# Final norm during the last expert, its own rows normed apart and written over, and one search for both token groups

## What is computed

```
def _expert_choice_ffn(h, w_router, w_gate, w_up, w_down):   # once for each token group
    cap = CAP_FACTOR * N // N_EXPERTS                        # 128 of 1024, 64 of 512; 16 experts
    aff = softmax(h @ w_router)
    gate, idx = lax.top_k(aff.T, cap)                        # each expert picks its tokens
    xe = h[idx]
    hid = silu(xe @ w_gate) * (xe @ w_up)                    # 1024 -> 2048
    ye = (hid @ w_down) * gate                               # 2048 -> 1024
    return zeros.at[idx].add(ye)

x = x + _expert_choice_ffn(rmsnorm(x, g_ffn), ...)
y = x * rsqrt(mean(x * x) + 1e-6) * g_final                  # final norm, every token
```

## Time and profile before

| what | value |
|---|---|
| time before, median of 3 runs | 2661.93 us (2661.03 to 2663.06) |
| profiled execution | 2664.18 us, span 2662.4 us |
| TensorE busy | 2515.5 us, 94% of the span |
| VectorE busy | 1731.1 us, 65% |
| ScalarE busy | 1486.1 us, 56% |
| GpSimd busy | 187.2 us, 7% |
| mean granted TensorE clock | 0.974 |
| moved by DMA | 536.65 MB, mean 202 GB/s |

### The profile page before, as it was taken

How to read it: one execution, slowest core, us unless ns; L and a number is a source line. 1 busy time by engine, 2 the same in 40 slices (tenths; PEclk the granted TensorE clock), 3 DMA queues, 4 the chain that set the end, 5 groups by cost and what they waited for, 6 DMA issues and landing times. The chain is left out here.

```text
span 2662.4 us, 42232 instructions
## 1 busy us (share of the span) xinstructions
PE 2515.5 (94%) x15538; PEld 2229.5 (84%) x15538; DVE 1731.1 (65%) x2743; ACT 1486.1 (56%) x2124; POOL 187.2 (7%) x268
## 2 busy tenths in 40 slices
PE   7999999979965999999999999999999999999992
PEld 5888866657755998999989999899998999989991
DVE  6354277765577766767667676676766767667675
ACT  4333277765543565655656556565565655656553
POOL 0000011000001010110101101011010110101100
PEclk9999999989987999999999999999999999999996
DMA  4332132235435676776767767677676776767765
GB/s 151 127 127 90 62 108 92 89 117 184 144 121 184 234 246 227 253 248 232 246 227 253 248 232 246 227 253 248 231 246 227 252 248 231 246 227 253 249 230 209
DMA packets 95484, 536.65 MB, mean 202 GB/s; under 512 B 10608, under 2 KB 15472, under 8 KB 44848
## 3 DMA queue, kind: packets, MB, share of 16 engines
q1 hardware_dynamic: 88016, 509.72, 54.2%
q0 software_dynamic: 7392, 25.96, 4.5%
HBM read 497.89 MB, written 37.75 MB: 201 GB/s over the span
## 5 line engine op out<-in xcount | busy, mean ns | idle before, releaser
L1413 DVE TENSOR_TENSOR ex_w_lo<-ex_w,ex_w_hi 128x2048 fp32r<-128x2048 f32 x387 | 887.0, 2292 | 471.1 <-ACT ex_w_hi L1366 471.1
L1366 ACT ACTIVATE ex_w_hi<-ex_w 128x2048 fp32r<-128x2048 f32 x387 | 739.2, 1910 | 232.2 <-PE ex_down_ps L1517 114.1
L1499 PE MATMUL ex_gate_ps<-ex_xt,ex_w_hi 128*128 128x384 f32 x2048 | 594.3, 360 | 1.5 <-DVE ex_xt L1419 1.5
L1499 PE MATMUL ex_up_ps<-ex_xt,ex_w_hi 128*128 128x384 f32 x2048 | 592.1, 359 | 0.0
L1501 PE MATMUL ex_gate_ps<-ex_xt,ex_w_lo 128*128 128x192 f32 x2048 | 513.8, 251 | 0.0
L1501 PE MATMUL ex_up_ps<-ex_xt,ex_w_lo 128*128 128x192 f32 x2048 | 512.7, 250 | 0.0
L1501 PEld LDWEIGHTS ex_gate_ps<-ex_xt,ex_w_lo 128*128 128x128 f32 x2048 | 392.5, 192 | 0.6
L1501 PEld LDWEIGHTS ex_up_ps<-ex_xt,ex_w_lo 128*128 128x128 f32 x2048 | 391.2, 191 | 0.0
L1499 PEld LDWEIGHTS ex_gate_ps<-ex_xt,ex_w_hi 128*128 128x128 f32 x2048 | 386.0, 188 | 2.3 <-issue 1.7
L1499 PEld LDWEIGHTS ex_up_ps<-ex_xt,ex_w_hi 128*128 128x128 f32 x2048 | 384.6, 188 | 0.0
L1386 ACT ACTIVATE ex_up_low<-ex_up_ps 128x384 f32<-128x384 f32 x128 | 63.0, 492 | 213.6 <-PE ex_up_ps L1501 213.6
(11 more groups left out here) (215 smaller groups left out, 4142.1 us busy)
## 6 DMA issues: line engine op xcount, KB each, us to landing
ex_w<-in_w_experts SPq DMA_DIRECT2D x387, 1024.0 KB, 4.8
pj_w<-in_w_in SPq DMA_DIRECT2D x54, 512.0 KB, 3.4
at_bias<-in_near_bias SPq DMA_DIRECT2D x8, 1536.0 KB, 8.1
pj_x<-in_x SPq DMA_DIRECT2D x12, 512.0 KB, 4.4
o_scratch<-at_o SPq DMA_DIRECT2D x24, 256.0 KB
mx_o<-o_scratch SPq DMA_DIRECT2D x12, 512.0 KB, 4.1
mx_x<-in_x SPq DMA_DIRECT2D x12, 512.0 KB, 4.6
acc_scratch<-mx_x SPq DMA_DIRECT2D x12, 512.0 KB, 5.4
```

Of the source, the lines that this page charges most:

```text
L1366: act.activation(w_hi[:, c % SLOTS, :], w[:, c % SLOTS, :], ACT.Copy).then_inc(hi_w, 1)
L1413: dve.tensor_tensor(w_lo[:, c % SLOTS, :], w[:, c % SLOTS, :], w_hi[:, c % SLOTS, :].bitcast(F32), ALU.subtract).then_inc(lo_w, 1)
L1499: nc.tensor.matmul(out[:, b, 0:2 * CAP], w_hi[:, slot, f], xt[:, k, :, :].rearrange("p h c -> p (h c)"), start=k == 0, stop=False)
```

## The change

It has four parts.

1. **Search.** The 6 sample rounds in `choose` take partitions 0 to 111, so the prompt's rows too, over 512 columns; the columns that the prompt lacks hold -2. Two rounds over the prompt's rows alone follow. `best` and `at` get 144 columns, the prompt's lists lie from column 80 on. The merge works on both groups in one instruction.
2. **First expert.** GpSimd starts its gathers after the first index operation; VectorE waits until both are issued (`ch.gathering`), splits chunk 0, makes the low halves of the gathered rows and only then splits chunks 1 and 2. `gathered` becomes `gathered_s` and `gathered_p`, and TensorE turns the sample rows when they alone are there.
3. **Last expert.** The loops run over 15 experts and the last one is written out. It turns and gathers no next rows. In it SP loads all 12 tiles of `acc` as they are without the last expert (from chunk 9, after the scatters of the expert before), in 8 slots, ScalarE squares them, VectorE norms them, SP stores them: a schedule by chunk (`FIN_...`).
4. **The last expert's own rows.** GpSimd gathers their `acc` rows into `x_s` and `x_p`. The two output halves are added to them rather than scattered, multiplied by the gain, squared by halves, scaled by their root, and scattered to `out` over what the tiles' stores wrote, after all stores have landed. The finish block is gone.

```diff
+LISTED = 8 * (EARLY + P_ROUNDS)
+SAMPLE_ROWS, ALL_ROWS, PROMPT_ROWS = (
+    (slice(0, SEG_AT + EXPERTS), S_SEG), (slice(0, SEG_ROWS), S_SEG), (slice(PROMPT_AT, SEG_ROWS), P_SEG))
...
-            pool.memset(route.rows[:, 0, :], 0.0).then_inc(ready, 1)
+            pool.memset(route.rows[:, 0, :], -2.0).then_inc(ready, 1)
...
-    for r in range(early, S_ROUNDS):
-        take_best(dve, route, ch.steps, r - early, False, r)
-    for r in range(P_ROUNDS):
-        take_best(dve, route, ch.steps, late + r, True, r)
+    for r in range(EARLY, rounds):
+        take_best(dve, route, ch.steps, r - EARLY, ALL_ROWS if r < S_ROUNDS else PROMPT_ROWS, r)
...
+    dve.tensor_tensor(route.gates[:], half(0, 0), half(0, 1), ALU.max).then_inc(ch.done, 1)
+    dve.tensor_tensor(ch.mine[:], half(0, 0), half(0, 1), ALU.is_ge).then_inc(ch.compared, 1)
+    dve.tensor_tensor(ch.span[:], half(1, 0), half(1, 1), ALU.subtract).then_inc(ch.compared, 1)
...
+    dve.tensor_tensor(route.index[:, :, 0:EXPERTS], ch.span[:], half(1, 1), ALU.add).then_inc(ch.done, 1)
+    dve.tensor_tensor(route.index[:, :, EXPERTS:], ch.span[:, :, 0:1], half(1, 1)[:, :, 0:1],
+                      ALU.add).then_inc(ch.last_index, 1)
...
+FIN_SLOTS, FIN_BATCH = 8, 6
+FIN_LOAD, FIN_STORE = 9, 19
+FIN_SQUARES = [5, 6, 7, 8, 9, 10, 13, 14, 16, 17, 18, 19]
+FIN_ROOTS = [11, 20]
+FIN_NORMS = [12, 13, 14, 15, 16, 17, 20, 21, 21, 22, 22, 23]
+FIN_LAST = [4, 5]
...
+            for c in range(W_CHUNKS):
+                load_w(LAST, c)
+                if c == FIN_LOAD:
+                    sp.wait_ge(y_free, LAST + START)
+                if 0 <= c - FIN_LOAD < FIN_SLOTS // 2:
+                    load_fin(2 * (c - FIN_LOAD))
+                    load_fin(2 * (c - FIN_LOAD) + 1)
+                if c >= FIN_STORE:
+                    store_fin(c - FIN_STORE)
+                    if c - FIN_STORE >= 2:
+                        load_fin(c - FIN_STORE - 2 + FIN_SLOTS)
+            for t in range(W_CHUNKS - FIN_STORE, TILES):
+                store_fin(t)
+                if t - 2 + FIN_SLOTS < TILES:
+                    load_fin(t - 2 + FIN_SLOTS)
...
+            for i in range(FIN_SLOTS):
+                pool.wait_ge(fin_moved[i], stored_at(TILES - 1 - (TILES - 1 - i) % FIN_SLOTS))
+            pool.wait_ge(rooted, 1)
+            pool.indirect_dma_start(d["out"], bass.IndirectOffsetOnAxis(last_row_s, 0),
+                                    fin[:, FIN_LAST[0], :], None).then_inc(last_out, 16)
+            pool.wait_ge(rooted, 2)
+            pool.indirect_dma_start(d["out"], bass.IndirectOffsetOnAxis(last_row_p, 0),
+                                    fin[0:P_CAP, FIN_LAST[1], :], None).then_inc(last_out, 16)
+            pool.wait_ge(last_out, 32)
...
             choose(dve, route, ch)
-
-            for c in range(AHEAD):
-                split(0, c)
+            dve.wait_ge(ch.gathering, 1)
+            split(0, 0)
             for i in range(FILLS):
                 low_x(0, i)
+            for c in range(1, AHEAD):
+                split(0, c)
...
+            def add_last(k):
...
+                dve.scalar_tensor_tensor(out=y_s[:, c], in0=y_ps[k][0], scalar=last_gate_s, in1=x_s[:, c],
+                                         op0=ALU.mult, op1=ALU.add).then_inc(added_s, 1)
+                dve.wait_ge(y_lowered, n)
+                dve.tensor_tensor(y_p_sum[:], y_ps[k][1][0:P_CAP, :], y_low[:], ALU.add).then_inc(y_summed, 1)
+                dve.wait_ge(y_summed, n + START)
+                dve.scalar_tensor_tensor(out=y_p[:, c], in0=y_p_sum[:], scalar=last_gate_p, in1=x_p[:, c],
+                                         op0=ALU.mult, op1=ALU.add).then_inc(added_p, 1)
...
+                dve.tensor_tensor(fin[:, FIN_LAST[0], c], y_s[:, c], gain[:, c], ALU.mult).then_inc(gained, 1)
...
+                inverse_root(dve, refined, len(FIN_ROOTS) * REFINE, last_ss[:], last_rt[:],
+                             [tmp[:, i, 0:2] for i in range(3)], last_rs[:], 1.0 / D)
+                dve.wait_ge(gained, 2 * HALVES)
+                last = [fin[:, FIN_LAST[0], :], fin[0:P_CAP, FIN_LAST[1], :]]
+                dve.tensor_scalar(last[0], last[0], last_rs[:, 0:1], None, ALU.mult).then_inc(rooted, 1)
+                dve.tensor_scalar(last[1], last[1], last_rs[0:P_CAP, 1:2], None, ALU.mult).then_inc(rooted, 1)
...
-            pe.wait_ge(gathered, 32)
+            pe.wait_ge(gathered_s, 16)
             turn_x(0)
             turn_x(1)
+            pe.wait_ge(gathered_p, 16)
             pe.wait_ge(lo_x, 1)
             turn_x(2)
```

More of the change, by code:

```diff
@@ L1376, in _, with expert @@
                 high_x(0, i)
-            with act.Fori(0, EXPERTS) as e:
+            def expert(e, last=False):
                 spans, halves = e * SPANS, e * HALVES
@@ new lines, in finish_norms @@
+            def finish_norms(c):
+                if c in FIN_ROOTS:
+                    b = FIN_ROOTS.index(c)
+                    tiles = slice(b * FIN_BATCH, (b + 1) * FIN_BATCH)
+                    dve.wait_ge(root, b + 1)
+                    inverse_root(dve, refined, b * REFINE, ss[:, tiles], rt[:, tiles],
+                                 [tmp[:, i, :] for i in range(3)], rs[:, tiles], 1.0 / D)
+                    if b == 0:
+                        dve.wait_ge(const_in, 32)
+                for t in range(TILES):
+                    if FIN_NORMS[t] == c:
+                        x = fin[:, t % FIN_SLOTS, :]
+                        dve.scalar_tensor_tensor(out=x, in0=x, scalar=rs[:, t:t + 1], in1=gain[:], op0=ALU.mult,
+                                                 op1=ALU.mult).then_inc(normed, 1)
@@ L1467, in _ @@
+            with dve.Fori(0, LAST) as e:
+                expert(e)
+            expert(LAST, True)
         @block.tensor
@@ L1607, in program @@
+            with pe.Fori(0, LAST) as e:
+                expert(e)
+            expert(LAST, True)
 def program(nc, d):
```

263 lines of the change are left out of this document (156 added, 107 removed).

## The result

The changed kernel takes **2616.27 us** (median of 4 runs, 2614.47 to 2617.07), the kernel before on the same chip 2662.49 us (2661.03 to 2663.29, 4 runs): a ratio of **0.9824, 95% interval 0.9811 to 0.9836**. The forecast was 2615.4 with a range of 2610 to 2623.

The account below looks back on a forecast made before the run. TensorE bounds the expert loop, so only the two ends can gain: 8.3 + 0.45 + 3.2 + 1.7 + 32.9 = 46.5 us off the profiled 2664.2 gives 2617.7, less 2.3 to the median, 2615.4; range 2610 to 2623.

Parts of the forecast that it names:

- Search, 8.3: Behind the last router tile: six prompt rounds of 1.38 us go, more partitions cost nothing; 8.3 us saved.
- Index arithmetic, 0.45: Before the first gather: six fewer comparisons and index operations of 0.08 us ahead of GpSimd's release; 0.45 us saved.
- First gathers, 3.2: Before the first expert: shorter gather issue beside idle VectorE, sample rows turned without awaiting prompt rows; 3.2 us saved.
- Rival (b): First gather's issue is long by itself, not from splits; only 1.9 us gained there, total 2618; chance 0.07.
- Turns, 1.7: Last expert: TensorE no longer turns rows for an expert that doesn't exist; 1.7 us saved.
- the last expert's extra work at 0: Last expert: added norms, squares and table loads fit the idle time of VectorE and ScalarE; no stall, bound 2 us.
- rival (a): Last expert: mixed reads and writes don't reach 360 GB/s, so DMA is late; total 2622 us; chance 0.11.
- DMA lateness, 0.3: Last expert: late transfers delay the last tile's square and the six norms behind the second root; 0.3 us, bounds 0 and 5.
- the second burst: Chunks 19 to 23 of the last expert: 9.4 MB in 22.7 us; 0.8 us late at 400 GB/s, 3.4 at 360.
- (d): Rival: stores beside weight loads cut the queue to 192 GB/s in the last expert; slower, 2676 us; chance 0.03.
- The tail, 19.0: From ScalarE's last output copy to the end: 19.0 us instead of 52.2, the drain last; 33.2 saved.
- Rival (c): At the end: GpSimd's drain isn't needed or is short; 5.3 us less, total 2610; chance 0.06.

Follow-up runs that it names:

- the control: The changed kernel itself, unedited, run again in the same rounds as the variant with both gains of the end; 2614.93 us, ratio 0.9821.
- SP's wait: Changed kernel with the wait for the last two scatters moved from GpSimd to SP; 2614.5 us, ratio 0.9817.
- doubled stores: Changed kernel with each of the twelve tile stores done a second time, to a scratch of its own; 2628.66 us in one run.
- the eight traces of that order: Traces of kernels with stores and batches as in the changed kernel and the norms in the last expert; the sum starts 0.12 to 0.94 us after ScalarE's copy.

## Why the prediction was right, and what its terms measured

**Search, 8.3.** 8.2 in the trace and 8.19 when undone alone. The step that more partitions cost nothing held: 2.18 a round over 112 of them.

**Index arithmetic, 0.45.** 0.4.

**First gathers, 3.2.** 3.0, and undone one by one 1.2 and 1.8. The first issue took 1.12 rather than the 0.97 of the earlier trace rows, and the rows landed 4.5 after it began (forecast 4.3). The mechanism of the first half was right, its means not quite: VectorE was to hold its splits until both gathers are issued. But it was released at 810.90, 0.27 after the first issue had begun and 1.15 before the second did: GpSimd's increment behind the second gather does not wait for the issues in front of it. So a split ran beside the second issue, which took 1.92. The opening part's sentence that VectorE waits until both gathers are issued is wrong in the same way. Only the first issue was guarded, and only the first was on the path; that the second landed later was hidden by the separate wait. Rival (b), an issue long by itself, is out.

How a split lengthens an issue shows again in the last expert of the changed kernel:

```profile
2503.25 2.29 DVE L1534 TENSOR_TENSOR ex_w_lo<-ex_w,ex_w_hi 128x2048 fp32r<-128x2048 f32 x1 [1.25 <-ACT ex_w_hi L1451]
...
2504.49 1.92 POOL L1406 DMA_INDIRECT ex_x_s<-acc_scratch,index  x1 [10.36 <-issue]
```

The issue ends at 2506.41, 0.87 after the split. In the control it begins 0.1 earlier in its split, takes 2.02 and ends 0.87 after it; with SP's wait 0.8 into the split, 2.37, 0.88 after it. So the issue's length follows from where in a split it begins, and its end is fixed by the split's: it is held until the split is over. The second first gather (0.78 behind) and the first one beside three splits (over at 811.89, 0.98 behind the first of them, which is over 2.29 after 808.62) fit; in the kernel before it is 1.01 (822.32 against 821.31). The Trainium skill, "SBUF — State Buffer", section "SBUF: two separate sides", has VectorE and GpSimd share one pair of ports under an exclusive lock, held to its end by whichever operation starts first; a VectorE operation with two SBUF inputs, as the split is, takes it only against a GpSimd operation that reads SBUF. These rows agree with it where the split is first, if an issue is such an operation, which no row says. Where the issue is first they show no lock: the split at 810.90 began inside the first issue and took 2.29 as ever.

**Turns, 1.7, and the last expert's extra work at 0.** 110.91 to 109.20, with no gap of TensorE. ScalarE's loads of tables came in chunks 11, 13 and 20, 1.28 each with the next operation behind them at once (2540.05, 2548.74, 2586.67). The Trainium skill, "ScalarE: Activation LUTs", section "What ACT_TABLE_LOAD costs", adds 1.38 us to each such load; no row here shows that part, and the last norm ended 0.66 after ScalarE's last copy, within the 1 us that I had given as a sign. What I had not asked was who stands behind ScalarE's squares. They wait for tiles (7.5 us in all), and the weight splits stand behind them. The doubled stores show it as the first thing to break, not the weight transfers on which rival (a) rested.

**DMA lateness, 0.3.** The norms held the sample half's sum until 0.58 after ScalarE's copy in the first profile, 0.12 to 0.94 in the eight traces of that order, 0.12 in the control; where they are done in time it starts 0.15 ahead of it, and the tail is 16.8 to 16.9. The 0.3 lies inside that spread. The sum had priced the second burst alone: the first, 8.4 MB in 18.2 us, asks for 461 GB/s, more than any row shows. It cost nothing, since ScalarE's squares wait for no tile before the one at 2566.52. The queues moved 374 and 375 GB/s in the second burst, between the 360 and the 400 of the estimate, so (a) did not come about, and (d), 192 GB/s, is far off.

**The tail, 19.0.** It is 17.4, and this is the term that was mis-sized, by three errors, one of which went against the other two. Counted from ScalarE's last copy:

| step | forecast | trace |
|---|---|---|
| sample rows scaled | 5.45 | 5.86 |
| first scatter's issue begins | 5.75 | 6.73 |
| second issue begins | 8.15 | 8.05 |
| scatters landed | 13.35 | 11.7 |
| drain over | 18.8 | 17.2 |

The start came 1.0 later than forecast: 0.4 by the norms (0.58 late, with a chain of 5.28 behind them for the 5.45 of the sum) and 0.57 by the 0.87 that an issue takes to start, where I had taken 0.30 from the earlier trace rows, the distance to an instruction that it did not wait for. The first issue took 1.01, not the 2.1 that I had from the earlier trace rows and a surcharge for VectorE; a scatter that only writes is issued faster than the 1.61 of one that adds. And the landing took 3.7 from the second issue's start to the drain (3.4 and 3.5 from each issue to its landing), below my lower bound of 4.4. The bound came from adding scatters, the nearest rows there were, and from them downwards I had allowed for too little. The Trainium skill, "DMA: Bandwidth & Descriptors", section "Anatomy of one DMA — SWDGE (gpsimd) path", has 2.0 us plus the bytes over 436 GB/s, 2.6 for these 256 KB. My estimate put that behind the issue; with the 0.91 that the trace shows for the issue it is 3.5, against the 3.7, and nearer than my estimate from rows.

The drain was forecast at 5.45, as the last thing, and is 5.451. Rival (c), no drain or a short one, is out for this block. What I had wrong about it is its start: I had placed it behind the landing because the earlier trace rows show it there. It runs from GpSimd's last own work, so with the wait for the landing moved to SP the two overlap, and 2.8 us of the tail were never necessary.

**Why the total came so near.** The profiled execution came out 1.9 under the forecast (2615.77 against 2617.7), by the tail. But it lies 0.5 under its median, where that of before had lain 2.3 above its own, and I had carried the 2.3 over: 0.9 is left between 2615.4 and 2616.27. So the nearness is in part luck.

**The two lines that no edit touches.** The router's end moved 0.8 and the first expert -0.5. The control shows both as differences from run to run: with the same code the first maximum stands at 789.11 and at 790.50, and the first expert takes 112.71 and 114.29. The first expert's length has two parts. From its first matmul on TensorE is granted 1.2 GHz (0.50) for 3.1 to 6.5 us before it gets 2.4; before that matmul it had nothing but the turns, with waits between them. By the granted clock that costs 1.6 to 3.2 us against full speed: 2.7 in the kernel before, 1.7 in the changed one. Less that cost the first expert takes 111.05 to 111.15 in twelve of the fourteen traces and 112.6 in two, the first profile of the changed kernel and that of SP's wait, the two that have 347 matmuls in 50 us where the others have 353 or 354. So in the first profile 1.0 was gained by the clock and 1.5 lost by the pace, which makes the -0.5; in the control the gain stands alone, at 1.1. The prediction had no term for either. What sets the pace in a run, and how long the half clock lasts, is open.

## What to carry to other kernels

Here a block in which GpSimd issued indirect DMAs ended with a drain of 5.3 to 5.5 us that runs from GpSimd's own last work. Let another engine wait for its last transfers, and where it can be, let GpSimd finish early; a scatter as the last thing of a kernel costs its landing and this drain (here 10.7 us with the issues).

When work is moved under a saturated engine, ask of each engine that takes it what stands behind the new instruction in its order. Here the new squares wait for DMAs, and the splits that feed TensorE wait behind them; that cover is thinner than the one counted in bytes. And a pause of TensorE can cost more than its length: behind 1.85 us of waiting came a stretch at the half clock that cost another 1.8, in the one run that had such a pause.

Work out a small effect from a stretch between two marks of the trace, not from totals: from the first issue to the first matmul, and from the sample half's sum to the end, the traces repeat within 0.3 us, where the totals of one kernel differ by 3 to 5. Other stretches don't: from ScalarE's last copy to that sum it was 0.12 to 0.94, so a second profile of the same kernel is needed before a gain of 0.6 is put down to an edit.

## What the runs showed of the hardware that I had not expected

- **GpSimd's drain hides.** 5.45 us behind a landing, record of 7.41 but 5.5 from the end of the last issue when SP waits, and 5.29 in the middle of the block when GpSimd is done early.
- **An issue has a start-up and a lock.** It begins 0.82 to 0.93 us after its data are there, if GpSimd waited, and beside a split that began before it, it ends 0.78 to 1.01 after that split does.
- **An increment behind an indirect DMA doesn't wait for its issue.** VectorE was released 0.27 us after the first of two issues began and 1.15 before the second.
- **A scatter that only writes is cheaper than one that adds:** issues of 1.01 and 0.91 against 1.61 and 1.44, and 3.7 from the second issue to the drain against 5.9.
- **TensorE's pace varies at a granted clock of 1.00:** 347 or 354 matmuls in the same 50 us of the first expert, with no gap, in two executions of one kernel; all of the 14 experts behind it take 110.91 us in both.
- **The half clock came behind a pause.** With doubled stores TensorE had 1.85 us without a matmul, and 1.0 after the matmuls had begun again 0.50 was granted for 3.3 us. The first expert starts with 3.1 to 6.5 us of it, behind the wait for the search and the gathers.
